# Linear attention inside a projection: level exponents from one kept cumulative sum instead of interval products

## The chip, the cores and the metric

The kernel runs on one core of a Trainium2 chip. The metric is the device time of one execution in microseconds, the median of repeated runs; lower is better.

## The reference, cut to what matters

The program is a stack of mixer layers. The change touches one of them, the gated linear attention of the even layer. Each of its 4 heads has keys of 64 and values of 128 features; a decay `log_a` per token and key feature; 512 tokens (256 of context, 256 latents), scanned forward and backward:

```
cum = cumsum(log_a)                                  # per chunk
rel = where(tri, cum[t] - cum[s], -inf)              # t >= s
att = einsum('bthk,bshk,btshk->bhts', q, k, exp(rel))
o   = einsum('bhts,bshv->bthv', att, v) + einsum('bthk,bhkv->bthv', q * exp(cum), state)
state = exp(c_end) * state + einsum('bshk,bshv->bhkv', k * exp(c_end - cum), v)
```

The exponent differs for each pair of tokens and each key feature, so it can't be applied after the product of queries and keys. `log_a` itself is the logarithm of a sigmoid, divided by 16, of a low-rank product.

## The kernel before, in words

Activations lie with features on the 128 partitions and the 512 tokens along the free axis; weights come from memory in blocks of eight 128x128 tiles (512 KB), through a ring of four buffers (`weight_ring`). ScalarE makes a block's high part (L363), VectorE its low part (L369), and TensorE multiplies high x high, high x low and low x high (L502), so that 8 tiles against 512 tokens are 24 matmuls. Up to four blocks of parts exist at a time.

**Modulation blocks** are weight blocks too, in the same ring. VectorE alone reads them: two passes over 128x1024 (L829). `STREAM` (L110 to L119) says in which order blocks stand in the ring; `spread_among` mixes modulation blocks into the blocks of a projection. `MOD_EVEN` says how many of the first layer's 48 go up to the end of the even input projection; the rest go into the even output projection. VectorE does a modulation block ahead of the low part of the block that follows it in the ring.

**The even input projection** (`even_projection`) has 31 items: item 0 the low-rank product, 1 to 4 queries and keys, 5 to 8 one round of values (four token groups side by side), 9 and 10 gates, 11 to 18 with a short convolution (two taps on VectorE, L671, done for two items at a time), 19 to 22 another round of values, and 23 to 30 the rest. ScalarE empties the banks (L608 and L609 before the taps, L1429 elsewhere).

**Beside it** runs the linear attention, `GlaSteps`, in four other banks. Its work stands in generators, one per engine. A generator yields a number; the engine goes on with it when its own program has reached that half item: position 2e is about the middle of item e on TensorE, and ahead of item e's own work on ScalarE and VectorE. So every engine has one fixed order, written by these positions. Semaphores tie the engines together; an engine that waits holds up all that stands behind it.

A chunk is 128 tokens. Pairs of tokens are treated in seven levels: in level l the chunk falls into blocks of 2^l tokens, and a pair belongs to the level at which its tokens lie in different halves of one block. For such a pair the exponent is the sum from the middle to the later token plus the sum from the earlier to the middle: a factor on the query times a factor on the key. The position of level l is `13 + 4 (l - 1)`, two items to a level. In the kernel before, a level is:
- at its position, TensorE multiplies the logarithms with a 0/1 matrix of intervals (`distances`, 32 matmuls of 128 columns, L1596), ScalarE takes the exponential of the four banks (L1702);
- one position later, VectorE multiplies queries and keys with them (L1774 to L1777), the four factor products;
- at position + 3, TensorE makes the score product (`scores`, 32 matmuls, L1587), and VectorE copies the scores into `att` where the level's mask holds (L1748, the masked copy).

The interval matrices and masks are made by GpSimd (L1543). Logarithms come first: TensorE makes the decays at position 6, VectorE clips them (L1752), ScalarE takes absolute value, exponential and logarithm (L1694, L1696, L1697), VectorE combines (L1758). After the levels, a product with triangular matrices gives the cumulative sums for queries and chunk ends.

Of the kernel before, what the change touches and what calls it, by code (L numbers as in the profile page):

```python
# [21 lines left out]
ALU = mybir.AluOpType  # L22
ACT = mybir.ActivationFunctionType
AX = mybir.AxisListType

P = 128
# [3 lines left out]
T = CTX + LAT  # L30
TT = T // P
# [7 lines left out]
GW = GH * GV  # L39
# [63 lines left out]
MOD_EVEN = 44  # L103
# [187 lines left out]
def mid(ap, n):  # L291

    return ap.unsqueeze(1).broadcast_to([ap.shape[0], n, ap.shape[1]])
# [1179 lines left out]
class GlaSteps(Beside):  # L1473
# [12 lines left out]
    N_INTERVALS = 2 * GLEVELS  # L1486

    def __init__(self, K, f, a2, gate_buffers):
# [3 lines left out]
        self.table = K.take(3 * GLEVELS + 2, P)  # L1492
        self.ss, self.rt = K.take(16), K.take(16)
        self.between, self.masks, self.strict = (self.table[:, a:b, :] for a, b in ((0, 14), (14, 21), (21, 23)))
# [6 lines left out]
        table = self.table.rearrange("p i t -> p (i t)")  # L1501
        self.keys = table[:, 0:4 * T].rearrange("p (c i) -> p c i", c=TT)
        self.on = table[:, 0:4 * T].rearrange("p (c v) -> p c v", v=GW)
# [4 lines left out]
        (self.tabled, self.decayed, self.absed, self.logged, self.z_read, self.la_made, self.scored, self.taken, self.dists,  # L1508
         self.exps, self.made, self.q_made, self.key_dists, self.key_exps, self.keyed, self.summed, self.updated,
         self.outs, self.squared, self.reduced, self.rooted, self.scaled, self.turned, self.silued) = K.counts(24)  # L1510
# [28 lines left out]
    def pool_steps(self, pool):  # L1539
# [8 lines left out]
        for l in range(1, GLEVELS + 1):  # L1548
# [3 lines left out]
            fwd, bwd, mask, one = (a.rearrange("p (b w) -> p b w", w=size)  # L1552
                                   for a in (self.between[:, 2 * l - 2, :], self.between[:, 2 * l - 1, :],
                                             self.masks[:, l - 1, :], ones))
# [4 lines left out]
            for out, first, second in (  # L1559
                    (fwd[:, :, late], from_middle, (half, -1, [[size, n], [1, half]])),  # L1560
                    (fwd[:, :, early], (-1, 1, [[-size, n], [-1, half]]), to_middle),
                    (bwd[:, :, early], (0, 1, [[-size, n], [-1, half]]), to_middle),
                    (bwd[:, :, late], from_middle, (half - 1, -1, [[size, n], [1, half]])),
# [4 lines left out]
            ins.then_inc(*self.tabled.up())  # L1568
        pool.affine_select(out=self.strict[:, 0, :], in_=ones, compare_op=ALU.is_ge, fill=0.0, base=-1, pattern=[[-1, P]],
# [8 lines left out]
    def tensor_steps(self, pe):  # L1578
# [12 lines left out]
        def distances(fwd, bwd):  # L1591
# [21 lines left out]
        for l in range(1, GLEVELS + 1):  # L1613
            yield self.level(l)
# [2102 lines left out]
```

## Time and profile before

| | us |
|---|---|
| median of 3 runs (1747.83 to 1751.97) | 1749.3 |
| profiled execution | 1752.12 |
| its span | 1750.4 |
| TensorE busy in the span | 1680.4 |
| VectorE busy | 1320.9 |
| ScalarE busy | 853.2 |
| GpSimd busy | 56.6 |

The span runs from the first to the last instruction of the core; the execution's own time is slightly more. A busy share is an average over stages. Each stage ends in a barrier on which all engines wait, so the engine that ends last in a stage sets its length.

### The profile page before, as it was taken

Reading aid. Unit: us, or ns where it says so; the run is one execution under the profiler, and the core shown is the slowest. Engines: PE = TensorE matmul, PEld = TensorE weight load, DVE = VectorE, ACT = ScalarE, POOL = GpSimd, SP = SyncE. Lnnn points to the kernel's source line nnn. Section 1 sums busy time; section 2 is a strip of 40 time slices with the busy share of each in tenths; the row PEclk is TensorE's granted clock in tenths of the full one; section 3 lists DMA queues with packets and bytes.
Section 4 is the critical chain, followed back from the end, with each engine's and each line's share of the span. In section 5 each row is a group of like instructions: output and inputs, shape, how many; then the busy total and the mean of one; then the engine's idle time right before and its main releaser. Section 6 shows DMA issues by size and latency. Waiting matters only on the chain. (4 is left out here: it accounts for less than half of the span.)

```text
span 1750.4 us, 26403 instructions
## 1 busy us (share of the span) xinstructions
PE 1680.4 (96%) x10206; PEld 1423.7 (81%) x10206; DVE 1320.9 (75%) x2484; ACT 853.2 (49%) x1481; POOL 56.6 (3%) x116
## 2 busy tenths in 40 slices
PE   5899999899999999999999998999999999999998
PEld 1688887677888888878888657988888988998998
DVE  3677874876999999979984688598875555765586
ACT  3723334746555542256654564333354567665542
POOL 0910000000000000000000000000000000000000
PEclk8899999999999999999999999999999999999999
DMA  8343431041322236744553334544455454444443
GB/s 323 133 155 112 140 124 49 1 143 68 115 96 97 96 98 215 242 143 146 183 182 121 94 100 149 171 155 153 150 196 191 151 175 147 131 133 133 145 157 109
DMA packets 70581, 246.03 MB, mean 141 GB/s; under 512 B 8031, under 2 KB 9752, under 8 KB 70072
## 3 DMA queue, kind: packets, MB, share of 16 engines
q1 hardware_dynamic: 68312, 241.52, 42.1%
q10 hardware_dynamic: 2080, 2.76, 0.5%
q8 instruction: 81, 1.33, 0.3%
q14 instruction: 44, 0.36, 0.1%
q0 software_dynamic: 64, 0.07, 0.0%
HBM read 242.87 MB, written 1.18 MB: 139 GB/s over the span
## 5 line engine op out<-in xcount | busy, mean ns | idle before, releaser
L502 PE MATMUL banks<-m,weights_high 128*128 128x256 f32 (+1 forms) x4144 | 980.8, 330 | 9.1 <-DVE weights_low L369 6.5
L502 PEld LDWEIGHTS banks<-m,weights_high 128*128 128x128 f32 x4144 | 698.6, 190 | 87.7 <-issue 9.8
L502 PE MATMUL banks<-m,weights_low 128*128 128x256 f32 (+1 forms) x2072 | 676.9, 327 | 0.0
L369 DVE TENSOR_TENSOR weights_low<-weight_ring,weights_high 128x1024 fp32r<-128x1024 f32 x293 | 355.4, 1224 | 199.4 <-ACT weights_high L363 198.6
L363 ACT ACTIVATE weights_high<-weight_ring 128x1024 fp32r<-128x1024 f32 x293 | 309.4, 1057 | 249.7 <-DMA weight_ring<-in_weights 141.7
L502 PEld LDWEIGHTS banks<-m,weights_low 128*128 128x128 f32 x2072 | 394.2, 190 | 33.9
L671 DVE SCALAR_TENSOR_TENSOR m<-m,columns 128x189 f32<-128x189 f32 (+4 forms) x504 | 199.5, 480 | 9.7 <-ACT m L609 9.6
L829 DVE SCALAR_TENSOR_TENSOR m<-weight_ring,m 128x1024 bf16<-128x1024 f32 x160 | 195.8, 1224 | 7.8 <-ACT m L808 2.5
L502 PE MATMUL banks<-m,weight_ring 128*128 128x256 f32 x704 | 152.1, 379 | 0.0
L502 PEld LDWEIGHTS banks<-m,weight_ring 128*128 128x128 f32 x704 | 133.7, 190 | 18.1
L608 ACT ACTIVATE m<-banks,columns 128x512 f32<-128x512 f32 (+1 forms) x76 | 58.3, 767 | 162.0 <-PE banks L502 157.0
L671 DVE SCALAR_TENSOR_TENSOR m<-m 128x189 f32<-128x189 f32 (+2 forms) x352 | 122.6, 425 | 10.2 <-ACT m L609 10.2
L502 PE MATMUL banks<-weights_high,m 128*128 128x512 f32 (+1 forms) x288 | 90.1, 389 | 8.1 <-ACT m L1429 7.0
L2782 ACT ACTIVATE m<-banks 128x256 f32<-128x256 f32 x74 | 28.6, 386 | 100.7 <-PE banks L502 94.3
L502 PEld LDWEIGHTS banks<-weights_high,m 128*128 128x128 f32 x288 | 54.0, 191 | 19.9 <-ACT m L1429 8.7
L608 ACT ACTIVATE m<-banks,columns,m 128x256 f32<-128x256 f32 x44 | 24.8, 564 | 90.8 <-PE banks L502 90.8
L609 ACT ACTIVATE m<-banks 128x512 f32<-128x512 f32 (+1 forms) x120 | 60.4, 504 | 0.0
L502 PE MATMUL banks<-weights_low,m 128*128 128x512 f32 (+1 forms) x144 | 55.2, 383 | 0.0
L452 PE MATMUL banks<-tri_f,identity 128*128 128x128 f32 x226 | 29.2, 287 | 11.6 <-PEq L1241 5.4
L452 PEld LDWEIGHTS banks<-tri_f,identity 128*128 128x128 f32 x226 | 27.5, 200 | 15.4 <-issue 13.8
L2612 DVE TENSOR_TENSOR m<-m 128x768 f32<-128x768 f32 x32 | 30.5, 953 | 11.2 <-ACT m L2693 11.2
L498 PE MATMUL banks<-m,weights_high 128*128 128x512 f32 (+1 forms) x96 | 35.6, 377 | 2.6 <-ACT m L945 2.5
(415 smaller groups left out, 1724.8 us busy)
## 6 DMA issues: line engine op xcount, KB each, us to landing
weight_ring<-in_weights SPq DMA_DIRECT2D x433, 512.0 KB, 3.7
m<-entering SPq DMA_DIRECT2D x32, 256.0 KB, 3.2
x<-in_tokens SPq DMA_DIRECT2D x2, 1024.0 KB, 9.3
m<-in_cmp_w SPq DMA_DIRECT2D x1, 2048.0 KB, 7.3
m<-in_cond SPq DMA_DIRECT2D x2, 512.0 KB, 7.0
out<-x ACTq DMA_DIRECT2D x8, 128.0 KB, 1.9
m<-in_rg_w ACTq DMA_DIRECT2D x1, 512.0 KB, 3.5
m<-in_spatial_w ACTq DMA_DIRECT2D x1, 512.0 KB
```

Of the source, the lines that this page charges most:

```text
L363: act.activation(K.w_hi[:, g % PARTS, :], K.ring[:, place % RING, :], ACT.Copy).then_inc(*K.high_done.up())
L369: dve.tensor_tensor(K.w_lo[:, g % PARTS, :], K.ring[:, PLACE[PRODUCT_BLOCKS[g]] % RING, :], K.w_hi[:, g % PARTS, :].bitcast(F32), ALU.subt ...
L452: pe.matmul(K.bank[:, bank, 0:P], K.ident[:], K.tri_f[:], start=True, stop=True)
L498: pe.matmul(out, lhsT, rhs, start=p.start and i == 0, stop=False)
L502: mm = pe.matmul(out, lhsT, rhs, start=p.start and i == 0, stop=p.stop and i == len(passes) - 1)
L608: act.activation(acc[:, i % ACC, 0:c.n], bank[:, 0:c.n], ACT.Identity, bias=c.bias, scale=c.centre)
L609: act.activation(raw[:, i % RAW, 0:c.n], bank[:, 0:c.n], ACT.Copy).then_inc(*free_act.up())
L671: ins = dve.scalar_tensor_tensor(o, shift(raw[:, i % RAW, 0:c.n]), w, o, ALU.mult, ALU.add)
L829: dve.scalar_tensor_tensor(self.unread, K.ring[:, place % RING, :], 1.0, self.cond[:, c, :], ALU.mult, ALU.mult, accum_out=K.mod[:, layer, ...
L2612: dve.tensor_tensor(w, w, mid(cb[:, g % 2, d, :], 2), ALU.mult).then_inc(*weighted.up())
L2782: act.activation(dest, bank[:, 0:LAT], func_of[func], scale=scale))])
```

## The change

TensorE makes the cumulative sums (matrices `tri_f`, `tri_b`) once, at level 1; ScalarE copies them from the banks into a kept tile `sums`. In each level VectorE subtracts from it its value in the middle of each block (forward: the last token of the early half, backward: the first of the late half), over 128x1024 for each direction. The difference has one sign in the late half and the other in the early one, so ScalarE takes the exponential in four pieces with a scale of 1 or -1. The final exponential reads the kept sums. The masked copy of a level moves behind the differences of the next. The decays' steps on ScalarE stand at three positions instead of one, the combination on VectorE at its own. The interval matrices go. `MOD_EVEN` is 40 instead of 44.

```diff
-MOD_EVEN = 44
+MOD_EVEN = 40
 ...
-        self.table = K.take(3 * GLEVELS + 2, P)
+        self.sums, self.table = K.take(4, T), K.take(GLEVELS, P)
 ...
         for l in range(1, GLEVELS + 1):                      # tensor_steps
-            yield self.level(l)
-            pe.wait_ge(*self.taken.at(l))
-            pe.wait_ge(*self.tabled.at(l))
-            pe.wait_ge(*self.la_made.at(1))
-            distances(self.between[:, 2 * l - 2, :], self.between[:, 2 * l - 1, :])
+            if l == 1:
+                yield self.level(l)
+                pe.wait_ge(*self.taken.at(l))
+                pe.wait_ge(*self.la_made.at(1))
+                sums(K.tri_f[:], K.tri_b[:])
             yield self.level(l) + 3
+            pe.wait_ge(*(self.taken.at(l) if l > 1 else self.sums_kept.at(1)))
             pe.wait_ge(*self.made.at(l))
             scores(self.factor[l % 2][:, 0, :, :], self.factor[l % 2][:, 1, :, :])
-        yield self.SUMS
-        pe.wait_ge(*self.taken.at(GLEVELS + 1))
-        distances(K.tri_f[:], K.tri_b[:])
 ...
-        yield self.DECAYS + 1                                # scalar_steps
+        yield self.DECAYS + 2
         act.wait_ge(*self.z_read.at(1))
         act.activation(e, self.banks(), ACT.Abs).then_inc(*self.absed.up())
+        yield self.DECAYS + 3
         act.wait_ge(*self.absed.at(1))
         link(act.activation(e, e, ACT.Exp, scale=-1.0))
+        yield self.DECAYS + 4
         act.activation(e, e, ACT.Ln, bias=K.small[:, 1:2], scale=1.0).then_inc(*self.logged.up())
-        for l in range(1, GLEVELS + 2):
-            yield self.SUMS if l > GLEVELS else self.level(l)
-            act.wait_ge(*self.dists.at(l))
-            act.wait_ge(*(self.made.at(l - 1) if l > 1 else self.la_made.at(1)))
-            act.activation(e, self.banks(), ACT.Exp).then_inc(*self.exps.up())
+        yield self.level(1)
+        act.wait_ge(*self.dists.at(1))
+        act.activation(self.sums, self.banks(), ACT.Copy).then_inc(*self.sums_kept.up())
+        for l in range(1, GLEVELS + 1):
+            yield self.level(l) + 1
+            act.wait_ge(*self.differenced.at(l))
+            for d in range(2):
+                decay = e[:, 2 * d:2 * d + 2, :].rearrange("p a (b w) -> p (a b) w", w=size)
+                for part, sign in ((late, 1.0 - 2.0 * d), (early, 2.0 * d - 1.0)):
+                    ins = act.activation(decay[:, :, part], decay[:, :, part], ACT.Exp, scale=sign)
+            ins.then_inc(*self.exps.up())
+        yield self.SUMS
+        act.wait_ge(*self.made.at(GLEVELS))
+        act.activation(e, self.sums, ACT.Exp).then_inc(*self.exps.up())
 ...
+        yield self.DECAYS + 5                                # vector_steps
         dve.wait_ge(*self.logged.at(1))
 ...
         for l in range(1, GLEVELS + 1):
-            yield self.level(l) + 1
+            yield self.level(l)
+            if l == 1:
+                dve.wait_ge(*self.sums_kept.at(1))
+            else:
+                dve.wait_ge(*self.made.at(l - 1))
+            for d, middle in enumerate((half - 1, half)):
+                decay, total = (a[:, 2 * d:2 * d + 2, :].rearrange("p a (b w) -> p (a b) w", w=size) for a in (e, self.sums))
+                ins = dve.tensor_tensor(decay, total, total[:, :, middle:middle + 1].broadcast_to([P, 2 * T // size, size]),
+                                        ALU.subtract)
+            ins.then_inc(*self.differenced.up())
+            if l > 1:
+                take_scores(l - 1)
+            yield self.level(l) + 2
             dve.wait_ge(*self.exps.at(l))
 ...
-            yield self.level(l) + 3
-            take_scores(l)
+        yield self.SUMS
+        take_scores(GLEVELS)
```

Three places show how instructions move. The first is VectorE in levels 4 and 5. L1774 to L1777 and L1793 to L1796 are the factor products, L1748 and L1754 the masked copy, L1779 the differences, L671 the taps, L829 a modulation block, L369 a low part. Before:

```order
L671 SCALAR_TENSOR_TENSOR m<-m,columns 128x2x255 x4
L829 SCALAR_TENSOR_TENSOR m,modulation<-weight_ring,m 128x1024 x2
L369 TENSOR_TENSOR weights_low<-weight_ring,weights_high 128x1024
L1774 TENSOR_TENSOR m<-m 128x32x16
L1775 TENSOR_TENSOR m<-m 128x32x16
L1776 TENSOR_TENSOR m<-m 128x32x16
L1777 TENSOR_TENSOR m<-m 128x32x16
L829 SCALAR_TENSOR_TENSOR m,modulation<-weight_ring,m 128x1024 x2
L369 TENSOR_TENSOR weights_low<-weight_ring,weights_high 128x1024
L1748 COPY_PREDICATED m<-m,banks 128x2048
L671 SCALAR_TENSOR_TENSOR m<-m,columns 128x2x255 x4
```

Now, the same stretch up to the factor products of level 5 and the taps behind them:

```order
L671 SCALAR_TENSOR_TENSOR m<-m,columns 128x2x255 x4
L1779 TENSOR_TENSOR m<-m 128x1024 x2
L1754 COPY_PREDICATED m<-m,banks 128x2048
L829 SCALAR_TENSOR_TENSOR m,modulation<-weight_ring,m 128x1024 x2
L369 TENSOR_TENSOR weights_low<-weight_ring,weights_high 128x1024
L1793 TENSOR_TENSOR m<-m 128x32x16
L1794 TENSOR_TENSOR m<-m 128x32x16
L1795 TENSOR_TENSOR m<-m 128x32x16
L1796 TENSOR_TENSOR m<-m 128x32x16
L829 SCALAR_TENSOR_TENSOR m,modulation<-weight_ring,m 128x1024 x2
L369 TENSOR_TENSOR weights_low<-weight_ring,weights_high 128x1024
```

Between taps and factor products there now stand two differences and the masked copy. The second place is ScalarE where the decays are made; L1429 empties a bank of queries or keys. Before:

```order
L363 ACTIVATE weights_high<-weight_ring 128x1024
L1429 ACTIVATE m<-banks 128x512
L1694 ACTIVATE m<-banks 128x2048
L1696 ACTIVATE m<-m 128x2048
L1697 ACTIVATE m<-m,small 128x2048
L363 ACTIVATE weights_high<-weight_ring 128x1024
L1429 ACTIVATE m<-banks 128x512
```

Now:

```order
L363 ACTIVATE weights_high<-weight_ring 128x1024
L1686 ACTIVATE m<-banks 128x2048
L1429 ACTIVATE m<-banks 128x512
L1689 ACTIVATE m<-m 128x2048
L363 ACTIVATE weights_high<-weight_ring 128x1024
L1691 ACTIVATE m<-m,small 128x2048
```

The last key item's bank is emptied behind the first of the three steps, no longer behind all. The third place is the first part of VectorE's work in the even output projection; L898 is the residual of one item, L1061 belongs to the sum of squares. Before:

```order
L898 SCALAR_TENSOR_TENSOR x<-banks,modulation,x 128x256 x2
L829 SCALAR_TENSOR_TENSOR m,modulation<-weight_ring,m 128x1024 x2
L369 TENSOR_TENSOR weights_low<-weight_ring,weights_high 128x1024
L898 SCALAR_TENSOR_TENSOR x<-banks,modulation,x 128x256 x2
L829 SCALAR_TENSOR_TENSOR m,modulation<-weight_ring,m 128x1024 x2
L369 TENSOR_TENSOR weights_low<-weight_ring,weights_high 128x1024
L898 SCALAR_TENSOR_TENSOR x<-banks,modulation,x 128x256 x2
L1061 TENSOR_TENSOR m<-m 128x512
```

Now:

```order
L829 SCALAR_TENSOR_TENSOR m,modulation<-weight_ring,m 128x1024 x2
L369 TENSOR_TENSOR weights_low<-weight_ring,weights_high 128x1024
L898 SCALAR_TENSOR_TENSOR x<-banks,modulation,x 128x256 x2
L829 SCALAR_TENSOR_TENSOR m,modulation<-weight_ring,m 128x1024 x4
L369 TENSOR_TENSOR weights_low<-weight_ring,weights_high 128x1024
L898 SCALAR_TENSOR_TENSOR x<-banks,modulation,x 128x256 x2
L829 SCALAR_TENSOR_TENSOR m,modulation<-weight_ring,m 128x1024 x2
L369 TENSOR_TENSOR weights_low<-weight_ring,weights_high 128x1024
L898 SCALAR_TENSOR_TENSOR x<-banks,modulation,x 128x256 x2
L1061 TENSOR_TENSOR m<-m 128x512
```

A modulation block and a low part now stand ahead of the first residual, and two blocks (x4) ahead of the next low part; over the stage there are eight blocks and nine low parts instead of four and eight.

## Rows read from the trace of the kernel before

**Rows 1.** Page, part 1: engine, busy us (share) and instructions.
```profile
PE 1680.4 (96%) x10206; PEld 1423.7 (81%) x10206; DVE 1320.9 (75%) x2484; ACT 853.2 (49%) x1481; POOL 56.6 (3%) x116
```
**Rows 2.** TensorE in order of time: start us, us, engine, line, operation [idle before <-releaser].
```profile
84.15 0.76 PE L502 MATMUL banks<-weights_high,m 128*128 128x512 f32 x1 [7.00 <-ACT m L1429]
...
87.28 0.63 PE L502 MATMUL banks<-weights_low,m 128*128 128x512 f32 x1
...
111.08 2.06 PE L1587 MATMUL banks<-m 64*128 64x128 f32 x32
...
149.84 3.74 PE L1596 MATMUL banks<-m 128*128 128x128 f32 x32
153.33 0.70 PE L502 MATMUL banks<-m,weights_high 128*128 128x512 f32 x2
...
212.62 2.06 PE L1587 MATMUL banks<-m 64*128 64x128 f32 x32
...
336.51 0.73 PE L2095 MATMUL banks<-m 128*128 128x129 f32 x4 [2.55 <-DVE m L2115]
```
**Rows 3.** Busy time by stretch; the number behind POOL's is the granted clock.
```profile
84.00:88.00 4.00, 3.85 (x9) 3.09 (x10) 3.97 (x6) 0.85 (x1) 3.93 (x4) 0.51 0.00 0
144.95:161.90 16.95, 16.95 (x114) 14.35 (x113) 14.72 (x20) 6.31 (x7) 0.00 (x0) 1.00 0.38 125
...
337.00:341.00 4.00, 4.00 (x21) 3.78 (x21) 3.77 (x11) 2.45 (x7) 0.00 (x0) 0.57 0.00 0
```
**Rows 4.** Grouped rows of 56 to 245 us: busy us, mean ns | idle before.
```profile
L1596 PE MATMUL banks<-m 128*128 128x128 f32 x224 | 26.1, 275 | 0.0
...
L1748 DVE COPY_PREDICATED m<-m,banks 128x2048 f32<-128x2048 int32 x7 | 17.3, 2472 | 2.0 <-PE banks L1587 2.0
...
L1702 ACT ACTIVATE m<-banks 128x2048 f32<-128x2048 f32 x8 | 15.1, 1882 | 32.9 <-PE banks L1596 32.9
...
L1454 ACT ACTIVATE m<-m 128x512 f32<-128x512 f32 x8 | 5.0, 626 | 0.0
...
L1787 DVE TENSOR_TENSOR m<-m 128x1024 f32<-128x1024 f32 x2 | 2.4, 1220 | 0.0
```
**Rows 5.** VectorE in order of time, level 4.
```profile
151.34 2.73 DVE L671 SCALAR_TENSOR_TENSOR m<-m,columns 128x510 f32<-128x510 f32 x4 [1.81 <-ACT m L609]
153.98 1.22 DVE L829 SCALAR_TENSOR_TENSOR m<-weight_ring,m 128x1024 bf16<-128x1024 f32 x1
...
156.47 1.23 DVE L369 TENSOR_TENSOR weights_low<-weight_ring,weights_high 128x1024 fp32r<-128x1024 f32 x1
157.61 0.69 DVE L1774 TENSOR_TENSOR m<-m 128x512 f32<-128x512 f32 x1
...
160.02 1.22 DVE L829 SCALAR_TENSOR_TENSOR m<-weight_ring,m 128x1024 bf16<-128x1024 f32 x1
```
**Rows 6.** VectorE in order of time, opening of the input projection.
```profile
59.80 1.28 DVE L829 SCALAR_TENSOR_TENSOR m<-weight_ring,m 128x1024 bf16<-128x1024 f32 x1 [2.54 <-ACT m L808]
...
74.30 2.28 DVE L1752 TENSOR_SCALAR m<-banks 128x2048 f32<-128x2048 f32 x1
```
**Rows 7.** ScalarE in order of time, the same place.
```profile
76.62 1.88 ACT L1694 ACTIVATE m<-banks 128x2048 f32<-128x2048 f32 x1 [3.25 <-DVE m L1752]
...
83.32 0.57 ACT L1429 ACTIVATE m<-banks 128x512 f32<-128x512 f32 x1
```
**Rows 8.** VectorE in order of time, output projection.
```profile
370.95 0.88 DVE L898 SCALAR_TENSOR_TENSOR x<-banks,modulation,x 128x256 f32<-128x256 f32 x2 [2.73 <-PE banks L502]
...
397.82 1.23 DVE L369 TENSOR_TENSOR weights_low<-weight_ring,weights_high 128x1024 fp32r<-128x1024 f32 x1 [0.92 <-ACT weights_high L363]
400.34 0.88 DVE L898 SCALAR_TENSOR_TENSOR x<-banks,modulation,x 128x256 f32<-128x256 f32 x2 [1.30 <-PE banks L502]
401.56 1.23 DVE L369 TENSOR_TENSOR weights_low<-weight_ring,weights_high 128x1024 fp32r<-128x1024 f32 x1 [0.34 <-ACT weights_high L363]
```

More of the change, by code:

```diff
@@ L1500, in __init__ @@
         self.qc = mo.rearrange("p (i t) -> p i t", t=T)
-        table = self.table.rearrange("p i t -> p (i t)")
-        self.keys = table[:, 0:4 * T].rearrange("p (c i) -> p c i", c=TT)
-        self.on = table[:, 0:4 * T].rearrange("p (c v) -> p c v", v=GW)
+        sums = self.sums.rearrange("p i t -> p (i t)")
+        self.keys = sums.rearrange("p (c i) -> p c i", c=TT)
+        self.on = sums.rearrange("p (c v) -> p c v", v=GW)
         la = self.la.rearrange("p c i -> p (c i)")
@@ L1551, in pool_steps @@
             early, late = slice(0, half), slice(half, size)
-            fwd, bwd, mask, one = (a.rearrange("p (b w) -> p b w", w=size)
-                                   for a in (self.between[:, 2 * l - 2, :], self.between[:, 2 * l - 1, :],
-                                             self.masks[:, l - 1, :], ones))
+            mask, one = (a.rearrange("p (b w) -> p b w", w=size) for a in (self.masks[:, l - 1, :], ones))
             from_middle = (-half, 1, [[-size, n], [0, half]])
@@ L1559, in pool_steps @@
             for out, first, second in (
[L1560 to L1563, printed above, removed]
                     (mask[:, :, late], from_start, to_middle),
@@ L1589, in scores, with sums @@
             mm.then_inc(*self.scored.up())
-        def distances(fwd, bwd):
+        def sums(fwd, bwd):
             for d in range(2):
@@ L1627, in tensor_steps @@
             if i == 0:
-                pe.wait_ge(*self.exps.at(GLEVELS + 1))
+                pe.wait_ge(*self.taken.at(GLEVELS + 1))
                 pe.wait_ge(*self.tabled.at(GLEVELS + 1))
@@ L1691, in scalar_steps @@
         act.preload_act_table_set(LOG_EXP)
-        yield self.DECAYS + 1
+        yield self.DECAYS + 2
         act.wait_ge(*self.z_read.at(1))
         act.activation(e, self.banks(), ACT.Abs).then_inc(*self.absed.up())
+        yield self.DECAYS + 3
         act.wait_ge(*self.absed.at(1))
         link(act.activation(e, e, ACT.Exp, scale=-1.0))
+        yield self.DECAYS + 4
         act.activation(e, e, ACT.Ln, bias=K.small[:, 1:2], scale=1.0).then_inc(*self.logged.up())
-        for l in range(1, GLEVELS + 2):
-            yield self.SUMS if l > GLEVELS else self.level(l)
-            act.wait_ge(*self.dists.at(l))
-            act.wait_ge(*(self.made.at(l - 1) if l > 1 else self.la_made.at(1)))
-            act.activation(e, self.banks(), ACT.Exp).then_inc(*self.exps.up())
+        yield self.level(1)
[3 more added lines that the diff above has]
+            yield self.level(l) + 1
+            size, half = 1 << l, 1 << (l - 1)
+            early, late = slice(0, half), slice(half, size)
+            act.wait_ge(*self.differenced.at(l))
[7 more added lines that the diff above has]
+        act.activation(e, self.sums, ACT.Exp).then_inc(*self.exps.up())
         yield self.KEYS[0]
```

8 lines of the change are left out of this document (5 added, 3 removed).

## The prediction, made before the changed kernel ran

> **What bounds the kernel now.** I read the page first, then TensorE's own rows and the busy time by stretch, then the grouped rows, and last the rows in order of time where the change works. The page has TensorE busy for 1680.4 of 1750.4 us and VectorE for 1320.9 [rows 1], so what counts is TensorE's queue. The change works in the even input projection (about 43 to 303 us) and, through the moved modulation blocks, in the even output projection (352 to 403 us). In the first, TensorE has one long wait, 7.00 us ahead of the value products; a matmul at 87.28, 3 us after it, still takes 0.63 us, and the granted clock is 0.51 from 84 to 88, against 1.00 in a level: 1.2 instead of 2.4 GHz [rows 2, 3]. From there TensorE is full. One level, from one score product to the next, is 16.95 us; 3.5 of them are the interval product (149.84 to 153.33), 2.0 the score product, and 11.4 two items of the projection, 5.6 to 5.7 each. VectorE is busy for 14.72 of the 16.95 [rows 2, 3]. Those 2.2 us of slack are the number to keep in mind.
>
> **TensorE's terms.** Seven groups of 32 interval matmuls leave its queue (of eight, one stays in another place), 3.5 us each (32 of the 224 matmuls in the grouped rows are 3.7 busy) [rows 2, 4]: 24.5 us if nothing else came last. A level without its group is 11.4 + 2.0 = 13.4.
>
> **VectorE's terms.** From start to start a modulation block takes 2.42 (2.49 with a wait of 0.07), a low part 1.14, the four factor products 2.41, the four taps of two convolutions 2.64 [rows 5]; the masked copy of scores 2.4 [rows 4]. New in each level are two differences over 128x1024. No row shows one with a broadcast operand; the nearest is the product of two such operands, 1.22 busy, with starts 1.14 apart where something follows at once [rows 4, 5]: 2.3 per level. Bounds: 2.0, if the broadcast side were free, to 3.4, if each cost 0.7 of a masked copy of 2048 (2.47). A level with convolutions is then 2.64 + 2.3 + 2.4 + 2.41 + 2 x (2.42 + 1.14) = 16.9 us: VectorE alone needs what TensorE took before. The four modulation blocks that leave the stage are 9.7 us.
>
> **ScalarE's terms.** An exponential over 128x2048, 1.88 us, becomes four over 128x512; an operation of that size is 0.63 busy [rows 4], some 0.53 apart: 2.2 us. Short strided runs are not in the rows; bounds 2.0 to 3.0. This hides behind the masked copy (2.4) and mostly a modulation block and a low part. A copy of the sums and a final exponential, 1.9 each, are added and replace the eighth.
>
> **What is late next.** A score product at position level + 3 waits for factor products which now stand at level + 2 of VectorE's program, one position later, with the differences and the masked copy of the level before ahead of them. Call M the end of the factor products in a level with convolutions. TensorE: scores 2.0, second half of the item 2.8. ScalarE empties the bank, 1.5 until the taps start (149.84 to 151.34) [rows 2, 5]. VectorE meanwhile does a modulation block and a low part (3.6) and waits 2.7. Then taps 2.64, differences 2.3, masked copy 2.4, modulation 2.42, low part 1.14, factor products 2.41: 6.3 + 13.3 = 19.6 us. TensorE has only 2.0 + 2.8 + 5.6 + 2.8 = 13.2 of work up to the next score product. So it stands for 6.4 us in each of these levels, and all that is behind the score product in its queue stands too.
> The clock follows such a stop: 0.51 after the 7.00 us, and after a wait of 2.55 us at 336.51 the stretch 337 to 341 still has 0.57 [rows 2, 3]. 3.5 us at half speed lose about 1.6, on the chain. So a round is 21.2 us.
> The Trainium skill, "TensorE: Matmul & The Clock Gate", section "HAM oscillation — how this bites in real kernels", says that a loop whose waits let the array fall back starts slowly every time round, so that the price is paid in each iteration. By that rule a round is 21.2 us, without it 19.6; the trace agrees as far as single stops go (0.51 after one).
>
> **The opening.** The fourth weight block is now split ahead of the normalisation, 1.0 us on ScalarE and 1.1 on VectorE; TensorE's first round sets its own pace, so this hides (uncovered it costs 1.0). VectorE starts on modulation 1.0 later than 59.80, but has three blocks and three low parts ahead of reading the decays instead of four: 60.8 + 3 x 3.56 + 1.6 of waits for high parts = 73.1 to 75.4, before 74.30 to 76.6 [rows 6]. ScalarE's absolute value ends at 77.4 and the bank of the last key item is emptied right behind it, at 78.0, not at 83.9 behind three steps [rows 7]. TensorE resumes at 78.0, not 84.15, with 1 us of wait and no slow restart. Seven steps of the value round (2.8 each), scores 2.0 and sums 3.5 bring it to 103.1; level 1 (sums at 94.7, copied 96.7, differences 99.1, exponentials 101.3, factor products 103.8) lets it go on at 103.9. Before it was 111.08 [rows 2]: 7.2 ahead. In levels 2 and 3, without taps, VectorE's round is 2 x 3.56 + 2.3 + 2.4 + 2.41 = 14.2 and TensorE's 13.4: score products at 118.2 and 132.4, the latter 144.95 before [rows 3]. 12.5 ahead.
> **Levels 4 to 7.** The first round starts on a fast clock, 19.7, the other three are 21.2: 152.1, 173.3, 194.5, 215.7; before, the last was at 212.62 [rows 2]. The four give back 15.6: 3.1 behind. Of the modulation blocks that left, those of levels 1 and 5 stood beside waits and buy nothing.
> **Rest of the stage.** Scores 2.0, slow restart 1.6 and a value step 2.8 end at 222.1. Before it was 212.6 + 2.0 + 2.9, a wait of 0.6 and the last sums product of 3.5: 221.6 to 221.7. A wait for a low part near 265 goes with VectorE's lighter load, 0.9, and one high part less ahead of the barrier is worth 0.7. The stage ends 1.2 earlier.
>
> **Output projection.** It gets four modulation blocks more and a low part that was done one stage ahead: 4 x 2.42 + 1.14 = 10.8 us on VectorE, whose queue had free 2.73 us before 370.95 and 0.92, 1.30 and 0.34 at the end [rows 8], 5.3 in all. 5.5 us are left and come to the end: the last residual, at 400.34 before, starts near 406, TensorE's last item ends about 3.5 later, and the barrier waits for VectorE. Bounds: 3, if one block finds cover that I don't see, to 8, if the new blocks find their weights late.
>
> **Sum.** -7.2 (opening, level 1) - 5.3 (levels 2, 3) + 15.6 (levels 4 to 7) - 4.3 (closing sums, low part, end) + 5.5 (output projection) = +4.3 us. The profiled execution took 1752.1 us around its span of 1750.4, 2.8 above the median of 1749.3. On the median: **1753.6 us**.
>
> **Rivals.**
> A, a cheap restart: the waits form but the clock stays up. For it: TensorE's waits under 1 us had no slow stretch behind them; against it, the two slow ones above. The four 1.6s go: 4.3 - 6.4 = -2.1, 1747.2 us.
> B, faster: the stop is 2 to 3 us per level instead of 6.4, because emptying, taps and differences overlap more than in my chain; each 3.5 us then stays mostly won and the sum is -5 to -10, 1742 us. At its far end TensorE never stands: -24.5 - 7.7 + 5.5 = -27, 1723 us. Against it: VectorE's 16.9 per level exceed TensorE's 13.4. It decides from a round under 17 us.
> C, more of the same: exponentials of 3.0 and differences of 3.4 put 1.5 on each of four rounds, and weights that come late 3 on the output projection: +13, 1762 us.
>
> **Chances.** Forecast 0.50, A 0.25, B 0.15, C 0.10. A measurement of this kernel can tell about 0.2% (3.5 us) from no change. The forecast divides into 0.38 slower and 0.12 within, A into 0.15 within and 0.10 faster; B is faster, C slower: faster 0.25, same 0.27, slower 0.48. The forecast's own range is 1750 to 1758; with the near parts of A, B and C it is 1741 to 1760.
>
> **What would show it.** Right: TensorE waits of about 6 us for the last factor product (L1796), one in each of levels 4 to 7, a granted clock near 0.5 behind them, rounds of 19 to 21 us; the 7.00 us down to about 1; in the output projection VectorE without a gap, its last residual 5 to 6 us later after the stage's start. Wrong: rounds under 17 us, a clock of 1.00 throughout, or an output projection of the old length.

## The result, and the profile after

The changed kernel takes 1759.0 us (median of 7 runs, 1755.7 to 1763.2), the kernel before 1749.4 beside it: a ratio of 1.0051, 95% interval 1.0041 to 1.0061, so 9.6 us slower by the medians and 8.9 by the ratio. The forecast was 1753.6, 4.3 slower: side and mechanism as predicted, the amount half of what came. 1759.0 lies 1 us above the forecast's own range (1750 to 1758) and inside the wider one (1741 to 1760). The profiled execution (1763.2, span 1761.4) is the slowest of the seven; its span is 11.0 above that of before, and the steps below add up to these 11.0.

Page, part 1, of the changed kernel: busy us (share) and instructions.

```profile
PE 1667.5 (95%) x9982; PEld 1410.0 (80%) x9982; DVE 1335.3 (76%) x2498; ACT 855.7 (49%) x1503; POOL 23.6 (1%) x60
```

TensorE is busy for 12.9 us less than in [rows 1], and the span is 11 us longer. The 224 interval matmuls that left were 26.1 us [rows 4]; about half of that comes back in matmuls that take longer, 6.9 in the four slow score products below. Its rows in order of time, changed kernel (start us, us, engine, line, operation, idle time before and what ended it); L1581 is the score product, L1587 of [rows 2]:

```profile
79.16 0.47 PE L502 MATMUL banks<-weights_high,m 128*128 128x512 f32 x1 [1.09 <-ACT m L1429]
...
105.52 2.06 PE L1581 MATMUL banks<-m 64*128 64x128 f32 x32 [1.10 <-DVE m L1796]
...
119.69 2.06 PE L1581 MATMUL banks<-m 64*128 64x128 f32 x32 [0.76 <-DVE m L1796]
...
133.94 2.06 PE L1581 MATMUL banks<-m 64*128 64x128 f32 x32 [0.81 <-DVE m L1796]
...
153.82 3.78 PE L1581 MATMUL banks<-m 64*128 64x128 f32 x32 [6.43 <-DVE m L1796]
...
175.54 3.79 PE L1581 MATMUL banks<-m 64*128 64x128 f32 x32 [6.43 <-DVE m L1796]
...
198.29 3.78 PE L1581 MATMUL banks<-m 64*128 64x128 f32 x32 [6.43 <-DVE m L1796]
206.69 0.47 PE L502 MATMUL banks<-weights_high,m 128*128 128x512 f32 x1 [1.56 <-ACT m L609]
...
219.92 3.79 PE L1581 MATMUL banks<-m 64*128 64x128 f32 x32 [4.73 <-DVE m L1796]
```

The 7.00 us of [rows 2] are 1.09. Rounds, from one score product to the next, are 14.2, 14.3, 19.9, 21.7, 22.8 and 21.6, against 16.95 before. In levels 4 to 7 TensorE waits for the last factor product (L1796), 6.43 us three times and 4.73 in level 7; behind each the 32 small matmuls take 3.8 us instead of 2.06. Busy time by stretch, changed kernel (columns as in [rows 3]):

```profile
133.94:153.82 19.88, 13.45 (x81) 10.85 (x81) 16.82 (x22) 6.50 (x10) 0.00 (x0) 0.93 0.31 111
153.82:175.54 21.72, 15.29 (x80) 12.59 (x81) 14.44 (x18) 7.54 (x12) 0.00 (x0) 0.81 0.21 73
...
150.00:157.00 7.00, 3.18 (x30) 3.21 (x32) 4.80 (x8) 0.00 (x0) 0.00 (x0) 0.57 0.52 173
171.00:181.00 10.00, 5.46 (x36) 4.98 (x37) 7.91 (x12) 0.89 (x1) 0.00 (x0) 0.52 0.47 164
```

Around two of the stops the granted clock is 0.57 and 0.52, that is, mostly 1.2 instead of 2.4 GHz. VectorE in one such round, changed kernel, the stretch of [rows 5]:

```profile
140.33 2.73 DVE L671 SCALAR_TENSOR_TENSOR m<-m,columns 128x510 f32<-128x510 f32 x4 [2.99 <-ACT m L609]
142.98 2.35 DVE L1779 TENSOR_TENSOR m<-m 128x1024 f32<-128x1024 f32 x2
145.25 2.50 DVE L1754 COPY_PREDICATED m<-m,banks 128x2048 f32<-128x2048 int32 x1
147.64 1.21 DVE L829 SCALAR_TENSOR_TENSOR m<-weight_ring,m 128x1024 bf16<-128x1024 f32 x1
...
150.04 1.22 DVE L369 TENSOR_TENSOR weights_low<-weight_ring,weights_high 128x1024 fp32r<-128x1024 f32 x1
151.18 0.69 DVE L1793 TENSOR_TENSOR m<-m 128x512 f32<-128x512 f32 x1
```

From the taps to the last factor product nothing waits: that is the chain of the prediction, link by link.

The stages' first TensorE instructions, before:

```profile
303.27 1.13 PE L2072 MATMUL banks<-tri_f,identity 128*128 128x128 f32 x8 [0.30 <-PEq L446]
...
352.49 2.02 PE L452 MATMUL banks<-tri_f,identity 128*128 128x128 f32 x16 [1.12 <-PEq L2041]
...
403.45 3.36 PE L452 MATMUL banks<-tri_f,identity 128*128 128x128 f32 x28 [0.30 <-PEq L446]
```

and after:

```profile
307.53 1.13 PE L2091 MATMUL banks<-tri_f,identity 128*128 128x128 f32 x8 [0.30 <-PEq L446]
...
355.26 2.02 PE L452 MATMUL banks<-tri_f,identity 128*128 128x128 f32 x16 [1.43 <-PEq L2060]
...
413.24 3.03 PE L452 MATMUL banks<-tri_f,identity 128*128 128x128 f32 x25 [0.30 <-PEq L446]
```

The input projection ends 4.3 later, the stage behind it gives back 1.5 (no instruction of it changed), and the output projection is 58.0 us instead of 51.0, 7.0 longer. 1.2 more come further on, again with the same instructions. In both places the granted clock differs at the same instructions. TensorE before:

```profile
346.80 4.14 PE L2095 MATMUL banks<-m 128*128 128x129 f32 x20 [1.74 <-DVE m L2115]
...
1432.48 1.96 PE L3168 MATMUL banks<-m 64*128 64x15 f32 x32 [1.21 <-ACT m L288]
```

and after:

```profile
350.81 2.50 PE L2114 MATMUL banks<-m 128*128 128x129 f32 x20 [1.06 <-DVE m L2134]
...
1440.38 2.86 PE L3187 MATMUL banks<-m 64*128 64x15 f32 x32 [1.20 <-ACT m L288]
```

The first of the two was slow before (granted clock 0.57 in the 4 us from its start) and is fast now (1.00); the second was fast (1.00) and is slow (0.61), and from it to the two matmuls of 24x24 (L3158, now L3177), the same work, 16.2 us pass instead of 13.0.

VectorE's residuals in the output projection, changed kernel, the stretch of [rows 8]:

```profile
401.27 0.87 DVE L898 SCALAR_TENSOR_TENSOR x<-banks,modulation,x 128x256 f32<-128x256 f32 x2
...
409.08 1.22 DVE L369 TENSOR_TENSOR weights_low<-weight_ring,weights_high 128x1024 fp32r<-128x1024 f32 x1 [0.92 <-ACT weights_high L363]
410.22 0.87 DVE L898 SCALAR_TENSOR_TENSOR x<-banks,modulation,x 128x256 f32<-128x256 f32 x2
```

The last residual stands 55.0 us behind the stage's first matmul (410.22 - 355.26), before 47.9 (400.34 - 352.49): 7.1. One wait of 0.92, for a high part, stayed.

### The profile page after: what moved, and what is told of

Its sections match the earlier page's. It is cut to its first block and busy times, and to the rows that moved or that the text cites. A ratio compares the mean times of both kernels' runs of the same rounds, so it can differ in the third digit from the quotient of the medians.

```text
span 1761.4 us, 25928 instructions
## 1 busy us (share of the span) xinstructions
PE 1667.5 (95%) x9982; PEld 1410.0 (80%) x9982; DVE 1335.3 (76%) x2498; ACT 855.7 (49%) x1503; POOL 23.6 (1%) x60
## 5 line engine op out<-in xcount | busy, mean ns | idle before, releaser
L369 DVE TENSOR_TENSOR weights_low<-weight_ring,weights_high 128x1024 fp32r<-128x1024 f32 x293 | 354.8, 1222 | 187.7 <-ACT weights_high L363 186.9
L671 DVE SCALAR_TENSOR_TENSOR m<-m,columns 128x189 f32<-128x189 f32 (+4 forms) x504 | 199.2, 471 | 23.4 <-ACT m L609 23.2
L829 DVE SCALAR_TENSOR_TENSOR m<-weight_ring,m 128x1024 bf16<-128x1024 f32 x160 | 195.5, 1222 | 8.1 <-ACT m L808 2.5
L671 DVE SCALAR_TENSOR_TENSOR m<-m 128x189 f32<-128x189 f32 (+2 forms) x352 | 122.6, 425 | 10.2 <-ACT m L609 10.2
L609 ACT ACTIVATE m<-banks 128x512 f32<-128x512 f32 (+1 forms) x120 | 60.3, 503 | 0.0
L1581 PE MATMUL banks<-m 64*128 64x128 f32 x256 | 23.4, 352 | 26.7 <-DVE m L1796 26.7
L1581 PEld LDWEIGHTS banks<-m 64*128 64x128 f32 x256 | 21.6, 257 | 29.9 <-issue 29.9
```

The source lines that it names most:

```text
L369: dve.tensor_tensor(K.w_lo[:, g % PARTS, :], K.ring[:, PLACE[PRODUCT_BLOCKS[g]] % RING, :], K.w_hi[:, g % PARTS, :].bitcast(F32), ALU.subt ...
L609: act.activation(raw[:, i % RAW, 0:c.n], bank[:, 0:c.n], ACT.Copy).then_inc(*free_act.up())
L671: ins = dve.scalar_tensor_tensor(o, shift(raw[:, i % RAW, 0:c.n]), w, o, ALU.mult, ALU.add)
L829: dve.scalar_tensor_tensor(self.unread, K.ring[:, place % RING, :], 1.0, self.cond[:, c, :], ALU.mult, ALU.mult, accum_out=K.mod[:, layer, ...
L1581: mm = pe.matmul(K.bank[:, B + 2 * half + i, j * P:j * P + P], k[r, pair, c * P:c * P + P], q[r, pair, c * P:c * P + P], start=True, stop= ...
```

## The experiments

Ten kernels ran, in three groups, each with runs of the kernel before on the same chip (medians 1750.4, 1749.8 and 1750.9). Ratios are to these. The last column is the difference of the ratio from the changed kernel's 1.0051, times 1749.4, so that groups can be compared.

| kernel | median us | ratio (95%) | against the changed kernel, us |
|---|---|---|---|
| changed, `MOD_EVEN` 44 | 1756.9 | 1.0034 (1.0022 to 1.0046) | -3.0 |
| before, `MOD_EVEN` 40 | 1755.3 | 1.0028 (1.0017 to 1.0039) | |
| before, decay steps spread | 1744.7 | 0.9958 (0.9944 to 0.9971) | |
| changed, wait filled | 1755.5 | 1.0027 (1.0013 to 1.0040) | -4.2 |
| changed, differences first | 1750.6 | 1.0004 (0.9994 to 1.0014) | -8.2 |
| changed, both first | 1740.1 | 0.9944 (0.9929 to 0.9959) | -18.7 |
| both first, `MOD_EVEN` 44 | 1734.2 | 0.9904 (0.9892 to 0.9917) | -25.7 |
| changed, late scores | 1736.1 | 0.9925 (0.9913 to 0.9937) | -22.0 |
| late scores, `MOD_EVEN` 44 | 1736.7 | 0.9913 (0.9893 to 0.9933) | -24.1 |
| the same, blocks placed later | 1741.3 | 0.9947 (0.9934 to 0.9960) | -18.2 |

**The parts alone.** First the four modulation blocks, in the changed kernel:

```diff
-MOD_EVEN = 40
+MOD_EVEN = 44
```

> The changed kernel with MOD_EVEN back at 44. My theory: in levels 4 to 7 of the input projection TensorE waits for a chain in VectorE's fixed order, and the four modulation blocks that left stood beside waits; in the output projection they stand in a full VectorE queue. So the output projection goes back to its length of before (about 7 us shorter than in the changed kernel) and the input projection grows by 0 to 2 us: 5 to 7 us faster than the changed kernel, about 1753. The rival, that VectorE's total load in the input projection sets the time and its order does not: 9.7 us more load there, the stage grows by 7 to 10 us, nothing is won in total, 1759 or more.

Measured -3.0, less than expected. Its profile has the output projection back at 50.9 us (358.04 to 408.89). The input projection, from its first matmul (42.43, in the changed kernel 43.98) to its end (308.08 against 307.53), is 2.1 longer: 1.9 in the opening, where TensorE waits 2.18 instead of 1.09 ahead of the value products and 2.16 instead of 1.10 at level 1, and nothing in levels 2 to 7. So the two touched stages give 5.0, the low end of what was expected; the stage in between, which the edit doesn't touch, was 2.2 longer. Then the same edit the other way, in the kernel before:

```diff
-MOD_EVEN = 44
+MOD_EVEN = 40
```

> The kernel before with MOD_EVEN 40 and nothing else. My theory: TensorE sets the input projection, so four blocks less do nothing there but the 0.9 us wait for a low part and the 0.7 us of the early high part; the output projection grows by 7 us. 5 to 7 us slower than before, 1755 to 1756. Rival: the four blocks find cover in the output projection: no change, 1749. It tells how much of the changed kernel's loss is the moved blocks and how much the levels.

Measured +4.9 by the ratio, just under the expected 5 to 7. In its profile the input projection ends 2.6 earlier (1.3 of it because it begins earlier) and the output projection is 7.0 longer, as after the change: the price of 7.0 is that of the four blocks alone. Third, the decay steps of ScalarE and VectorE alone, in the kernel before:

```diff
-        yield self.DECAYS + 1
+        yield self.DECAYS + 2
 ...
+        yield self.DECAYS + 3
 ...
+        yield self.DECAYS + 4
 ...
+        yield self.DECAYS + 5
```

> The kernel before with only the steps of the decays spread out (positions on ScalarE and VectorE). My theory: the wait of 7.00 us ahead of the value round falls to 1 to 1.5, and the slow restart (1.6 us) goes with it. As all else in this stage is TensorE's own work, that stays won: 7 to 8 us faster than before, 1742. Rival: it is given back, because VectorE's combination of the logarithms comes later and the first levels wait for it: 0 to 3 us faster.

Measured -7.3 by the ratio (interval -9.8 to -5.1), as expected. TensorE, this kernel:

```profile
78.60 0.77 PE L502 MATMUL banks<-weights_high,m 128*128 128x512 f32 x1 [2.05 <-ACT m L1429]
...
85.83 2.06 PE L1587 MATMUL banks<-m 64*128 64x128 f32 x32
...
105.36 2.06 PE L1587 MATMUL banks<-m 64*128 64x128 f32 x32
```

The wait is 2.05 instead of 7.00, but the slow restart did not go: the first matmul takes 0.77 us and the granted clock is 0.58 from 78.6 to 82.6. From the end of the wait to the first score product it is 7.2 us, as before (7.4), where the changed kernel needs 5.7 for the same work. Level 1 comes at 105.36, close to the changed kernel's 105.52, but this execution began the stage at 41.86 and not at 43.98. From the stage's first matmul to level 1 it is 67.8 us before, 63.5 here and 61.5 in the changed kernel: the spread decays give 4.3 of the 6.3. The other 2.0 came with the four blocks that left; with them back (`MOD_EVEN` 44 above) it is 63.5 again. The kernel is faster than the kernel before with nothing else changed.

**Stop or clock.** In levels 4 to 7 of the changed kernel TensorE fills most of the wait with matmuls whose result is not used:

```diff
+            if l > 3:
+                for _ in range(WARM):                        # 24
+                    pe.matmul(K.bank[:, B, 0:P], K.ident[:], K.tri_f[:], start=True, stop=True)
```

> The changed kernel with 24 small matmuls on TensorE ahead of the wait for the factor products, in levels 4 to 7; they write a bank that the scores then overwrite. They do no useful work and fill about 5 us of the wait of 6.4. My theory: each round of levels 4 to 7 is 19.6 us of chain plus what a slow restart costs on it (2.1 to 3.1 in the changed kernel's trace). With TensorE kept at work the granted clock stays near 1.00 and the rounds are 19.6 to 20: 7 to 9 us faster than the changed kernel, about 1751. Rival: the clock is not what makes the rounds 21.7 to 22.7 us but waits on ScalarE and VectorE: no change or, as the fill stands ahead of the scores, a little slower.

Busy time by stretch, this kernel:

```profile
132.30:152.09 19.79, 19.07 (x129) 16.25 (x129) 16.74 (x22) 6.50 (x10) 0.00 (x0) 1.00 0.31 105
152.09:171.87 19.78, 19.06 (x128) 16.24 (x128) 14.44 (x18) 7.54 (x12) 0.00 (x0) 1.00 0.26 80
```

The clock stays at 1.00 and the rounds are 19.8, the chain without its slow restart (predicted 19.6). So in the changed kernel the clock costs the rounds of 21.7, 22.8 and 21.6 another 1.8 to 3.0, and the chain the rest. Measured -4.2 by the ratio, where about -8 was expected: two rounds gained 1.9 and 3.0, but in level 7 the fill could begin only at 209.00, behind a masked copy, and held up the score product itself (a round of 22.9 for 21.6). Behind level 7, where the fourth slow restart stood, the profile gives 3.1 more: 84.5 us to the end of the stage (214.55 to 299.09) instead of 87.6. The stage is 6.4 shorter in all, 2 more than the times show.

**The order on VectorE.** Only the differences of levels 4 to 7 ahead of the taps (the masked copy stays behind them):

```diff
-            yield self.level(l)
+            yield self.level(l) - (l > 3)
 ...
+            if l > 3:
+                yield self.level(l)
             if l > 1:
                 take_scores(l - 1)
```

> The changed kernel with only the two differences of levels 4 to 7 moved ahead of the taps on VectorE; the masked copy stays behind the taps, the load of VectorE and TensorE is the same. Theory (a dependent chain from one factor product to the next sets the round; the differences, 2.3 us, are one link): VectorE does a modulation block, a low part and the differences (5.9) while TensorE and ScalarE finish the item's bank (2.0 + 2.8 + 1.5 = 6.3); then taps 2.64, masked copy 2.4, modulation 2.42, low part 1.14, factor products 2.41: 17.3 per round, with a slow restart of about 2 still on the chain, 19 instead of 21.5. TensorE waits for L1796-like factor products of about 4 us instead of 6.4. Time 9 to 12 below the changed kernel, about 1748. Rival (VectorE's load of 16.9 per round or the emptying of banks sets the round, not the order): rounds stay at 20 to 22, time within 3 of the changed kernel.

Measured -8.2, a little less than the 9 to 12 expected. TensorE, this kernel:

```profile
148.66 3.79 PE L1581 MATMUL banks<-m 64*128 64x128 f32 x32 [4.14 <-DVE m L1798]
...
169.01 3.79 PE L1581 MATMUL banks<-m 64*128 64x128 f32 x32 [4.15 <-DVE m L1798]
...
189.41 3.79 PE L1581 MATMUL banks<-m 64*128 64x128 f32 x32 [4.15 <-DVE m L1798]
```

The stop is 2.3 shorter, the length of the two differences. The first round (from 131.07) is 17.6, predicted 17.3; the next three, which start with a slow restart, 20.4, where 19 was expected with 2 for the restart: it costs 2.8. Same engines, same load, another order: the chain is what counts. With the masked copy in front as well:

```diff
-            yield self.level(l)
+            yield self.level(l) - (l > 3)
```

> The changed kernel with differences and masked copy of levels 4 to 7 moved ahead of the taps on VectorE. Theory: what VectorE does from one factor product to the next no longer waits for a bank: modulation and low part 3.56, differences 2.3, masked copy 2.4, taps 2.64 (bank ready at 6.3 to 8 against 8.3), 2.42, 1.14, 2.41 = 16.9 per round, VectorE without a gap, and TensorE's slow restart no longer on the chain. Four rounds 68 instead of 86 us: 15 to 18 below the changed kernel, about 1742. TensorE still waits about 3.5 us per level. Rival (the slow clock behind each stop sets the round): rounds stay above 19 and the gain under 9, 1750 or more.

Measured -18.7, a little more than the 15 to 18 expected. Busy time by stretch, this kernel, its four rounds:

```profile
132.62:149.43 16.81, 13.45 (x81) 10.84 (x81) 16.74 (x22) 6.50 (x10) 0.00 (x0) 1.00 0.40 129
149.43:166.21 16.78, 15.00 (x81) 12.39 (x81) 14.55 (x18) 7.55 (x12) 0.00 (x0) 0.90 0.28 95
166.21:183.05 16.84, 15.06 (x81) 12.36 (x81) 16.77 (x22) 7.55 (x12) 0.00 (x0) 0.90 0.38 122
183.05:199.85 16.80, 15.12 (x81) 12.24 (x81) 16.73 (x22) 7.02 (x12) 0.00 (x0) 0.90 0.45 144
```

Rounds of 16.8, the 16.9 of VectorE's own work, which is without a gap in three of the four (in the second, with one modulation block fewer, it waits 0.38 for the scores and 1.81 for the taps' bank). TensorE still stops (3.36, then 1.78 twice) and restarts slowly (clock 0.90), but hardly on the chain now. 67.2 us instead of 86.0 for the four rounds is 18.8. The score product of level 7 is fast here, so what lies behind it is another 3.0 shorter (84.6 against 87.6), and the stage is 22.0 shorter in the profile, 241.5 against 263.6. The times show 18.7; in the profile the stage behind it, with the same instructions, is 2.2 longer than in the changed kernel.

**The order on TensorE.** VectorE as in the changed kernel, the score products of levels 4 to 7 half an item later:

```diff
-            yield self.level(l) + 3
+            yield self.level(l) + 3 + (l > 3)
```

> The changed kernel with only TensorE's score products of levels 4 to 7 one position (half an item, 2.8 us) later; VectorE's order is as in the changed kernel. Theory: the stop in front of the score product no longer holds up the half item whose bank the taps wait for. The end of that item, 1.5 of emptying, taps 2.64, differences 2.3, masked copy 2.4, modulation 2.42, low part 1.14 and factor products 2.41 are 14.8, less than VectorE's 16.9 per round: the same round as with both first by another way, 16.9, without touching VectorE. 12 to 17 below the changed kernel, about 1744. Rival (the wait moves along with the score product and nothing is won): waits of 3.5 to 6 at the new place, rounds above 19, 1755 or more.

Measured -22.0, more than expected. TensorE, this kernel:

```profile
152.54 2.93 PE L1581 MATMUL banks<-m 64*128 64x128 f32 x32 [3.65 <-DVE m L1796]
...
167.46 2.06 PE L1581 MATMUL banks<-m 64*128 64x128 f32 x32
...
183.76 3.38 PE L1581 MATMUL banks<-m 64*128 64x128 f32 x32 [2.84 <-DVE m L1796]
...
200.56 3.14 PE L1581 MATMUL banks<-m 64*128 64x128 f32 x32 [1.96 <-DVE m L1796]
```

The first round, from level 3 at its old place (132.64), is 19.9, the next are 14.9, 16.3 and 16.8, and at each of these score products half an item (2.8) more of the projection is done: the item whose bank the taps wait for is no longer behind the stopped score product, and VectorE is again the bound. The stage is 241.9 us, the same as with both first (241.5). That this kernel measured 3.3 lower lies in stages with the same instructions, and the intervals overlap. So the chain breaks on either engine: by the score product on TensorE, or by differences and masked copy together on VectorE; the differences alone only shortened it.

**With the four blocks back.** `MOD_EVEN` 44 in both of these, and in the last also another order in the ring:

```diff
-    + spread_among(blocks_of("mod0")[MOD_FIRST:MOD_EVEN], blocks_of("even_in")[TOGETHER:]) \
+    + spread_among(blocks_of("mod0")[MOD_FIRST:MOD_FIRST + 11], blocks_of("even_in")[TOGETHER:19]) \
+    + spread_among(blocks_of("mod0")[MOD_FIRST + 11:MOD_EVEN], blocks_of("even_in")[19:]) \
```

> As both first, with MOD_EVEN 44: four modulation blocks back in the input projection. Theory: output projection back at its old length (7 shorter: 50.7 instead of 57.7); the blocks' 9.7 us on VectorE in the input projection fall in the opening and in a VectorE-bound stretch, where they now cost up to 2.4 each (1 to 5 in all): 2 to 6 below both first, about 1738, faster than the kernel before by 10 or more. Rival (VectorE is so full in the levels that each block costs there what it saves in the output projection): same as both first, 1742.

Measured 0.9904, 7.0 below both first and 16.8 below the kernel before: the lowest time of this study, though its interval overlaps those of late scores with 40 and with 44. It is 9.4 below the kernel with the spread decays alone (0.9958): so much the differences give in their best order. TensorE, this kernel:

```profile
153.05 3.79 PE L1581 MATMUL banks<-m 64*128 64x128 f32 x32 [3.37 <-DVE m L1796]
...
170.83 2.06 PE L1581 MATMUL banks<-m 64*128 64x128 f32 x32 [1.77 <-DVE m L1796]
...
187.65 2.06 PE L1581 MATMUL banks<-m 64*128 64x128 f32 x32 [3.37 <-DVE m L1796]
```

The output projection is 50.9 instead of 58.0, but the input projection, from its first matmul on, is 6.0 longer than in both first (247.5 against 241.5), where 1 to 5 was expected. Only 0.9 of it is in the rounds of the levels. 3.4 are in the opening: the wait ahead of the value products is 0.8 longer and has a slow restart of 1.6 behind it, and the wait at level 1 is 1.1 longer. The last 1.6 are behind level 7. So the stages that the edit touches give 1.1 of the 7.0, as the rival has it; the rest lies in stages with the same instructions, in the profiles 2.2 between the two projections and 3.8 behind the second.

> As late scores, with MOD_EVEN 44 (four modulation blocks back in the input projection). Theory: the output projection becomes 7 us shorter, as it did between both first and both first with 44 (7.0 by the ratios), and in the input projection the blocks cost 1 to 3 where VectorE is full: 4 to 6 below late scores, about 1731. Rival: with late scores TensorE waits less, so each block in the full stretch from 140 to 210 us costs its 2.4 on the end: no gain, 1736.

Measured 0.9913, 2.1 below late scores, with intervals that overlap: the rival held. In its profile the output projection is 50.9 us, 7.1 shorter, and the input projection 7.3 longer (42.89 to 292.06, against 42.09 to 283.96): 3.3 up to level 1, 2.4 in the rounds, 1.6 behind them.

> As late scores with 44, and the 28 modulation blocks of the input projection placed otherwise in the ring: 11 among the weight blocks of items 3 to 18, 17 among those of items 19 to 30, instead of evenly. Nothing else differs. Theory: VectorE sets the rounds of levels 1 to 7 (16.8 in levels 4 to 7, no gap from 100 to 210 us) and has idle time behind them (about 25 of 40 us from 250 to 290 in late scores). One block less in two of three levels takes 2.4 us off each such round, down to TensorE's 13.4: levels 4 to 7 are 5 to 8 shorter, levels 1 to 3 and the opening 1 to 3, and the later blocks fit: 5 to 10 below late scores with 44, about 1724. Rival (the blocks are only paid later, at the end of the stage where linear attention's closing steps also stand on VectorE, or weights come late there): within 3 of late scores with 44.

Measured 0.9947, 5.9 slower than the even placement: the forecast fell, and so did its rival (within 3). VectorE makes low parts, and the modulation blocks ahead of them, some blocks before their item. So the denser part of the ring was already worked off from behind level 6 on. By VectorE's rows, levels 2 and 4 lost a block each, levels 3, 5 and 6 none, and level 7 has three instead of two. The opening is 2.9 shorter, as expected; levels 2 to 6 are not. TensorE, this kernel (its lines are one further):

```profile
185.71 2.06 PE L1582 MATMUL banks<-m 64*128 64x128 f32 x32 [1.78 <-DVE m L1797]
...
205.11 3.78 PE L1582 MATMUL banks<-m 64*128 64x128 f32 x32 [6.01 <-DVE m L1797]
...
251.41 0.32 PE L1930 MATMUL banks<-identity,m 36*128 36x36 f32 x1 [2.90 <-ACT m L1924]
```

The round of level 7 is 19.4, one modulation block (2.6 with its wait) more than 16.8, and a stop of 2.90 appears at 251. The largest loss is behind level 7: 91.7 us to the end of the stage instead of 85.0. The edit missed its aim, but the round of level 7 shows the bound once more: a block put into a VectorE-bound round costs its full length.

## Why the prediction was right or wrong, step by step

All numbers from the two profiled executions; the sum is +11.0, predicted +4.3.

- **Opening and level 1**: -7.2 predicted; 111.08 became 105.52, -5.6. The stage began 0.7 later (TensorE's work ahead of it, not part of the change); the other 0.9 are 0.4 up to the end of the wait and 0.5 between it and level 1. Wait of 1 us and no slow restart as predicted. That the block which left level 1 "buys nothing" was wrong: with it TensorE waits 2.16 there, without it 1.10.
- **Levels 2 and 3**: -5.3 predicted, -5.5 measured; rounds of 14.2 as worked out from VectorE's durations.
- **Levels 4 to 7**: +15.6 predicted, +18.3 measured (86.0 against 67.7). The stop was 6.4 predicted, 6.43 measured. This is the first mis-sized term: the restart. It was priced at 1.6 from the two slow stretches of [rows 2, 3]. From the score product's start to the taps (L671) it is 6.4 us with the clock kept up (152.09 to 158.47) and 8.2, 9.3 and 8.2 in the changed kernel: 1.8, 2.9 and 1.8. What runs at half speed right behind this stop are 32 dependent small matmuls, and they take 1.7 more by themselves. The rest, 0.2 per round, is the chain, 19.8 and not 19.6; the stop's length alone does not set the price: behind three equally long stops the granted clock is low for about 4 us, twice, and for nearly 6 in the round of 22.8. Rival A (a cheap restart) is out for this kernel: the clock fell at every one of these stops. Its opposite came.
- **The rule on loops**: the Trainium skill ("TensorE: Matmul & The Clock Gate", section "HAM oscillation — how this bites in real kernels") says that a loop whose waits let the clock fall pays the slow start in every iteration. The trace agrees, three rounds of 21.6 to 22.8 against 19.8 in the kernel that fills the wait. In both first with 44 it agrees in part: only the first of its four stops (3.37, 1.77, 3.37 and 1.68 us) has a slow start behind it.
- **Differences and exponentials**: 2.3 predicted, 2.35 with starts 2.27 apart; four exponentials 2.2 predicted, 2.20 to 2.34. A broadcast operand in the subtraction changed nothing. The masked copy 2.50 as before. Rival C's prices fell.
- **Rest of the stage**: -4.3 predicted, -3.0 measured (90.65 became 87.61). The same term again: the restart behind level 7 was priced at 1.6, and the three kernels whose level 7 is followed by a fast start, also with 40, need 84.5 to 84.6 from there on, 3.1 less. The wait for a low part near 265, said to go (0.9), stayed: 0.89 at 271.09, as before. A wait not foreseen, 1.56 for ScalarE's emptying (L609) at 206.69, cost nothing: the wait for L1796 behind it is 4.73 instead of 6.43.
- **Output projection**: +5.5 predicted, +7.0 measured. This is the second mis-sized term. Of 10.8 us of new work on VectorE I had taken off all 5.3 of its gaps; 3.7 were absorbed. The 0.92 for a high part stayed, and was never free: it waits for a high part of ScalarE, which is late as before. The other 0.7 is not traced. The kernel before with this edit alone shows the same 7.0.
- **Outside**: +1.2 and -1.5 in stages that the change doesn't touch, and not in the forecast. They go with the places at which the granted clock is low, which differ between the two profiles (4.14 against 2.50 us, 1.96 against 2.86, shown above). The medians say +9.6 where the profiles say +11.0.
- **Rival B** fell as a forecast for this kernel (no stop of 2 to 3 us), but its sign, "a round under 17 us", is what the reordered kernels show: with the chain broken the rounds are VectorE's 16.8, and the time is 1740.1. That this is near its 1742 is chance: B had each level's 3.5 us mostly won, and the rounds gained only 0.15 on 16.95.

What the change lost is its order, not its idea. Differences in place of interval products cost TensorE nothing and VectorE 2.3 us a level; put between the taps and the factor products they lengthened a chain through three engines beyond the round.

Still open is a part of the small amounts. The step of `MOD_EVEN` from 40 to 44 measured -3.0, -7.0 and -2.1 us in three surroundings, where the lengths of the two touched stages in the profiles say -5.0, -1.1 and +0.2. The rest lies in stages whose instructions are the same. The one between the two projections takes 47.7 us in five of the twelve profiles and 48.9 to 50.0 in the others: in those of 47.7 its last group of 20 small matmuls takes 2.50 us, in the two of 49.9 and 50.0, at half clock, 4.67. So the clock moves at least a part of it; what decides whether it falls behind a given short wait isn't shown. The 18.7 and 22.0 of the two reorderings are well above these amounts.

## What to carry to other kernels

Work taken from the full engine is won only if no cycle through the other engines is longer than what is left: before such a change, go once round from one hand-over to the same one a loop later, engine by engine, and put what doesn't depend on the bank in front of what waits for it. Here that was one position in one program, 18.7 us. A stop inside such a cycle is to be priced with what runs behind it at half clock, and a gap counts as cover only if nothing later releases it.

## What the runs showed of the hardware that was not expected

- A slow restart costs more than an earlier, longer stop had suggested: 6.43 us of waiting took 1.8 to 2.9 us from what followed, and 4.73 us ahead of level 7 took 3.1, where about 1.6 had been worked out from the slow stretches of before. 32 matmuls of 64x128 took 3.8 us instead of 2.06.
- Whether the clock falls is not fixed by the stop alone. In both first with 44 a stop of 3.37 us was followed once by score products of 3.79 us and once of 2.06; in both first one of 1.78 by 3.67. Ahead of the value products, the same work took 5.7 us behind waits of 1.09 and 2.18, and 7.2 to 7.3 behind waits of 1.88, 2.05 and 2.54. And the same 1.2 us wait late in the program has 32 matmuls of 64x15 in 1.96 us behind it before the change and in 2.86 after.
- 24 unused matmuls of 128 columns in a wait of 6.4 us kept the clock at 1.00 throughout the levels, and shortened the rounds from 21.7 and 22.8 to 19.8.
